# Second gate in three PSUM banks, three score slots in the dilated attention, and a transposition moved into the gate

## The chip, the cores and the metric

The kernel runs on one core of one Trainium2 chip as one launch of one program. The metric is the device time in microseconds; lower is better. Five engines work side by side, each through its own instructions in the order in which they are written, and wait for one another through counting semaphores: TensorE (PE in the profile; its weight loads are PEld), VectorE (DVE), ScalarE (ACT), GpSimd (POOL) and SyncE (SP), which issues most DMAs. TensorE writes only into PSUM, which has eight banks of 128 partitions by 512 floats.

## The reference

One inference step of a decoder layer for a prompt of 512 tokens and 8 samples of one token. All inputs go through one input projection, whose columns feed two attentions and four gates. The part that matters here is the dilated attention of the prompt (4 heads of 64, three patterns) and the gates beside it:

```python
h = _rms(x, norm_w) * (1 + scale[:, None]) + shift[:, None]
zq, zkv, zd, ga, gb, ma, mb, ... = split(h @ w_in)       # ga: 512 columns, gb: 256
...
for g, (win, dil) in enumerate(DIL_PATTERNS):            # (128,1), (512,4), (2048,16)
    s = einsum('bgnqhe,bgnkhe->bgnhqk', qb, kx) * DIL_SCALE
    s = where(band & has_prev, s, -inf)
    m = s.max(-1); e = exp(s - m[..., None]); l = e.sum(-1)
    acc = einsum('bgnhqk,bgnkhe->bgnqhe', e, vx)
o_b = _combine(stats).reshape(B, S, B_WIDTH)             # weighted by the softmax denominators
ya = (o_a * silu(ga)) @ w_pa
yb = (o_b * silu(gb)) @ w_pb
merged = sigmoid(ma) * ya + sigmoid(mb) * yb
y = x + res_gate * (merged @ w_out)
```

The 32 pages of each sample's cache, which the second half of the run works on, are not touched here.

## The kernel before

Every engine's instructions are written out by hand, in one order; semaphores carry the rest. The prompt half is a list of stages (STAGES). Each result tile of a stage has a running number, its item; item `idx` goes to PSUM bank `idx % 7`, and `wait_bank` lets TensorE write it once item `idx - 7` has been read out. Bank 7 is for odd jobs.

A projection (`block_of`) runs over chunks of 128 rows of the weight. Each chunk is loaded by SP into one of four raw slots, split by ACT (L620) and POOL (L931) into a high and a low part in one of three slots, and multiplied with the four tiles of 128 tokens and the tile of samples: three matmuls for each prompt tile, two for the samples, 14 in all per chunk. The gates are GA (512 columns) and GB (256 columns), of 8 chunks each.

Around the change the order on TensorE is: GA; the transposition of the third pattern's queries and keys (`heads_turned(2)`, stage TE, four items of four transposes); GB; the dilated attention (`pair_attention`); then the merge gates (MA0 and on). GA's tiles are read out by DVE (`mix`, L1927), which multiplies them with their sigmoid from ACT. TE's items are copied by ACT (`heads_in_order(2)`), GB's by ACT too.

The dilated attention has 16 jobs (PAIR_JOBS), each two heads of one tile of 128 queries: eight near jobs (first pattern; the first two have one block of keys, the others two), then eight far ones. A job n passes through:

- `qk(n)`, TensorE (L1255): scores of both heads, each into a bank of its own;
- `masks_max(n)`, DVE (L1895, L1900): adds the mask, takes the maximum, leaves the scores in `pair_probs`;
- `exp(n)`, ACT (L696);
- `tr(n)`, TensorE (L1266): transposes of the probabilities into a bank of PAIR_TURNED;
- `pt_copy(n)` (L469): that bank copied to `PT`, by DVE for even n and by ACT for odd n;
- PV(n), TensorE (L1297): probabilities times values, into a bank of PAIR_OUT;
- `finish(n)`, DVE (L1908): the result copied out.

Score slots, turned banks and output banks are two each. A turn of TensorE's loop is `tr(n + 1)`, `qk(n + 2)`, PV(n); a turn of DVE's is `masks_max(n + 1)`, `pt_copy(n)` if n is even, `finish(n - 1)`; a turn of ACT's is `exp(n + 1)`, `pt_copy(n)` if n is odd. `qk(0)` stands inside GB ahead of its chunk 5; `qk(1)` follows GB, since its banks hold GB's first two tiles.

Of the kernel before, what the change touches and what calls it, by code (L numbers as in the profile page):

```python
# [25 lines left out]
P = 128  # L26
# [65 lines left out]
FIRST = {}  # L92
# [47 lines left out]
_gb = [(ITEM["GB"] + t) % BANKS for t in range(BANKS)]  # L140
PAIR_SCORES, PAIR_OUT, PAIR_TURNED = ((_gb[5], _gb[6]), (_gb[0], _gb[1])), (_gb[3], _gb[4]), (7, _gb[2])
# [13 lines left out]
def turned_bank(chunk):  # L155

    return 6 + chunk % 2 if chunk < N_MLA_CHUNKS else PAIR_TURNED[(chunk - N_MLA_CHUNKS) % 2]
# [12 lines left out]
def trunk_step(nc, x_prompt, x_sample, cache_mla, cw0, cw1, cw2, page_table, c_prompt, c_sample, b_ada,  # L170
# [4 lines left out]
    with ctx:  # L175
# [154 lines left out]
        pair_p = v3(put("pair_probs", [P, 2 * 512], W + 18432), 2, 512)  # L330
# [272 lines left out]
        def _(act):  # L603
# [23 lines left out]
            def bank(idx, w, n=P, start=0):  # L627
                return ps[start:start + n, idx % BANKS, 0:w]
# [57 lines left out]
            def pair_attention():  # L686

                def exp(n):
                    near, i, hp, nb = PAIR_JOBS[n]
                    act.wait_ge(masked, N_MLA + n + 1)  # L690
                    for hh in range(2):
                        h = 2 * hp + hh
                        p = pair_p[:, n % 2, 256 * hh:256 * hh + nb * P]
# [319 lines left out]
        def _(pe):  # L1013
# [13 lines left out]
            def block_of(name, first, tiles, hi=None, lo=None, small=None, wait_h=False, ahead_of=None):  # L1027

                f, nk, w = FIRST[name], COUNT[name], WIDTH[name]
                for k in range(nk):  # L1030
# [8 lines left out]
                    for n, t in enumerate(tiles):  # L1039
# [3 lines left out]
                        out = ps[:, idx % BANKS, 0:w]  # L1043
                        st, en = k == 0, k == nk - 1
# [3 lines left out]
                        else:  # L1048
# [3 lines left out]
                            last = mm(out, lo[:, k, c], bh, start=False, stop=en)  # L1052
# [15 lines left out]
            def transposes(idx, parts, n_in=P):  # L1068

                wait_bank(idx)  # L1070
                for col, rows_out_, src in parts:
                    last = nc.tensor.transpose(ps[0:rows_out_, idx % BANKS, col:col + n_in], src, ident[0:n_in, 0:n_in])
                last.then_inc(z_done, 1)
# [165 lines left out]
            heads_turned(2, ITEM["TE"])  # L1239

            def pair_attention():
# [3 lines left out]
                def qk(n):  # L1245
                    near, i, hp, nb = PAIR_JOBS[n]
                    if n >= 2:
                        pe.wait_ge(masked, N_MLA + n - 1)
                    banks = PAIR_SCORES[n % 2]
# [9 lines left out]
                def tr(n):  # L1259
                    nb, c = PAIR_JOBS[n][3], N_MLA_CHUNKS + n  # L1260
                    pe.wait_ge(exp_done, N_MLA + n + 1)
                    if n >= 2:
                        wait_pt(pe, c - 2)
                    for q in range(2 * nb):
                        o = 256 * (q // nb) + P * (q % nb)
                        last = nc.tensor.transpose(ps[:, PAIR_TURNED[n % 2], q * P:(q + 1) * P], pair_p[:, n % 2, o:o + P], ident)  # L1266
# [12 lines left out]
                for n, (near, i, hp, nb) in enumerate(PAIR_JOBS):  # L1279
                    if n < last_job:  # L1280
                        tr(n + 1)
                    if n + 2 <= last_job:
                        qk(n + 2)
                    if n >= 2:
                        pe.wait_ge(o_done, N_MLA + n - 1)
# [5 lines left out]
                    for hh in range(2):  # L1291
                        h = 2 * hp + hh
                        for b in range(nb):
# [3 lines left out]
                            last = mm(ps[:, PAIR_OUT[n % 2], 64 * hh:64 * hh + 64], PT[:, c % 3, o:o + P], v_rows,  # L1297
# [207 lines left out]
        def _(dve):  # L1505
# [378 lines left out]
            def pair_attention():  # L1884

                def masks_max(n):
# [3 lines left out]
                    if n >= 2:  # L1890
                        dve.wait_ge(trp_done, N_MLA_CHUNKS + n - 1)
                    m = 4 * (n % 2)
                    msk = masks[:, M_ALL - w:M_ALL] if near else class_mask
                    for hh in range(2):
                        last = v.tensor_tensor_reduce(out=pair_p[:, n % 2, 256 * hh:256 * hh + w],  # L1895
                                                      in0=ps[:, PAIR_SCORES[n % 2][hh], 0:w], in1=msk, scale=1.0, scalar=NEG,
# [6 lines left out]
                def finish(n):  # L1903
# [4 lines left out]
                    v.tensor_copy(out, ps[:, PAIR_OUT[n % 2], 0:2 * DH].rearrange("p (h e) -> p h e", h=2)).then_inc(o_done, 1)  # L1908
# [366 lines left out]
```

## Time and profile before

| | |
|---|---|
| median of 3 runs | 1371.1 us (1368.76 to 1372.58) |
| profiled execution, its own time | 1372.51 us |
| its span, first to last instruction | 1370.7 us |
| mean granted TensorE clock | 0.913 of 2.4 GHz |
| busy share: PE, PEld, DVE, ACT, POOL | 89%, 73%, 52%, 36%, 19% |
| chain that ended last: PE, DVE, issue, ACT, DMA, POOL | 57%, 19%, 8%, 5%, 5%, 4% |

The profiled execution took 1.8 us beyond its span, and 1.4 us more than the median. The busy shares are means over stages with different limits. TensorE's clock has two levels, 2.4 and 1.2 GHz; a granted clock of 1.00 is the upper one, 0.50 the lower.

### The profile page before, as it was taken

Reading aid. Unit: us, or ns where it says so; the run is one execution under the profiler, and the core shown is the slowest. Engines: PE = TensorE matmul, PEld = TensorE weight load, DVE = VectorE, ACT = ScalarE, POOL = GpSimd, SP = SyncE. Lnnn points to the kernel's source line nnn. Section 1 sums busy time; section 2 is a strip of 40 time slices with the busy share of each in tenths; the row PEclk is TensorE's granted clock in tenths of the full one; section 3 lists DMA queues with packets and bytes.
Section 4 is the critical chain, followed back from the end, with each engine's and each line's share of the span. In section 5 each row is a group of like instructions: output and inputs, shape, how many; then the busy total and the mean of one; then the engine's idle time right before and its main releaser. Section 6 shows DMA issues by size and latency. Waiting matters only on the chain.

```text
span 1370.7 us, 22960 instructions
## 1 busy us (share of the span) xinstructions
PE 1219.1 (89%) x7616; PEld 998.1 (73%) x7616; DVE 715.8 (52%) x1657; ACT 495.2 (36%) x1159; POOL 254.7 (19%) x252
## 2 busy tenths in 40 slices
PE   5987758998897899999987999998999899997986
PEld 1277647786786678778765998988999899997431
DVE  4137887456865233030322676766676667676422
ACT  1133334332243333322322554545454545453010
POOL 0023330048865012333431000000000000000000
PEclk9989857999999657999998999999999999998579
DMA  8622010031242102233264310323232323225005
GB/s 262 220 77 72 23 41 1 13 81 47 73 127 77 31 23 71 77 101 85 71 199 159 96 31 22 88 62 88 61 86 64 88 61 83 66 75 184 1 20 166
DMA packets 79398, 112.24 MB, mean 82 GB/s; under 512 B 8627, under 2 KB 50756, under 8 KB 79293
## 3 DMA queue, kind: packets, MB, share of 16 engines
q1 hardware_dynamic: 76214, 101.59, 25.8%
q0 software_dynamic: 1440, 5.11, 1.0%
q10 hardware_dynamic: 1648, 4.23, 0.8%
q8 instruction: 65, 1.06, 0.3%
q14 instruction: 31, 0.25, 0.1%
HBM read 105.21 MB, written 5.68 MB: 81 GB/s over the span
## 4 chain that ended last, share of the span: by engine, by line
PE 57%; DVE 19%; issue 8%; ACT 5%; DMA 5%; POOL 4%; SPq 2%; ACTq 0%; DVEq 0%; POOLq 0%
PE ps L1376 18%; PE ps L1050 5%; PE ps L1051 5%; PE ps L1052 5%; PE ps L1357 5%; DVE ssq L2106 3%; PE ps L1065 3%; PE ps L1402 3%; DMA raw<-in_w_ada 2%; ACT cT_hi L850 2%; PE ps L1422 2%; PE ps L1212 1%; PE ps L1255 1%; POOL tmp L946 1%; PE ps L1266 1%
## 5 line engine op out<-in xcount | busy, mean ns | idle before, releaser
L931 POOL TENSOR_TENSOR wlo<-raw,whi 128x512 fp32r<-128x512 f32 (+3 forms) x148 | 172.1, 1165 | 459.8 <-ACT whi L620 459.6
L1376 PE MATMUL ps<-wq_hi,cT_hi 128*128 128x260 f32 x1024 | 217.8, 294 | 0.5 <-ACT sq L879 0.5
L1050 PE MATMUL ps<-whi,hT_hi 128*128 128x512 f32 (+3 forms) x512 | 190.3, 372 | 30.4 <-POOL wlo L931 19.2
L2106 DVE TENSOR_REDUCE ssq<-sq 128x8 f32<-128x512 f32 x256 | 172.6, 682 | 66.6 <-ACT sq L879 64.5
L1376 PE MATMUL ps<-wq_hi,cT_lo 128*128 128x260 f32 x1024 | 206.3, 283 | 0.0
L1376 PE MATMUL ps<-wq_lo,cT_hi 128*128 128x260 f32 x1024 | 206.0, 282 | 0.0
L620 ACT ACTIVATE whi<-raw 128x512 fp32r<-128x512 f32 (+3 forms) x148 | 83.3, 564 | 316.5 <-PE ps L1047 246.3
L1052 PE MATMUL ps<-whi,hT_lo 128*128 128x512 f32 (+3 forms) x512 | 185.8, 363 | 0.0
L1051 PE MATMUL ps<-wlo,hT_hi 128*128 128x512 f32 (+3 forms) x512 | 185.7, 363 | 0.0
L1376 PEld LDWEIGHTS ps<-wq_hi,cT_hi 128*128 128x128 f32 x1024 | 157.6, 190 | 1.1 <-ACT sq L879 1.1
L1376 PEld LDWEIGHTS ps<-wq_hi,cT_lo 128*128 128x128 f32 x1024 | 158.2, 189 | 0.0
L1376 PEld LDWEIGHTS ps<-wq_lo,cT_hi 128*128 128x128 f32 x1024 | 158.1, 189 | 0.0
L879 ACT ACTIVATE sq<-ps 128x512 f32<-128x512 f32 x256 | 152.0, 594 | 0.0
L1050 PEld LDWEIGHTS ps<-whi,hT_hi 128*128 128x128 f32 x512 | 99.2, 194 | 56.1 <-POOL wlo L931 25.3
L2024 DVE TENSOR_TENSOR cT_lo<-ps,cT_hi 128x1024 fp32r<-128x1024 f32 x64 | 78.3, 1224 | 103.3 <-ACT cT_hi L850 103.3
L1052 PEld LDWEIGHTS ps<-whi,hT_lo 128*128 128x128 f32 x512 | 98.9, 193 | 14.6
L1051 PEld LDWEIGHTS ps<-wlo,hT_hi 128*128 128x128 f32 x512 | 99.4, 194 | 13.4
L877 ACT ACTIVATE s_latent<-ps 128x8 f32<-128x8 f32 x256 | 45.2, 177 | 165.1 <-PE ps L1376 165.1
L850 ACT ACTIVATE cT_hi<-ps 128x1024 fp32r<-128x1024 f32 x64 | 65.7, 1027 | 83.5 <-PE ps L1359 83.4
L1357 PE MATMUL ps<-tab,cn 128*128 128x128 f32 x512 | 69.6, 280 | 17.5 <-DVE s_rotary L2103 10.1
L1357 PEld LDWEIGHTS ps<-tab,cn 128*128 128x128 f32 x512 | 55.5, 142 | 29.1 <-issue 24.6
L633 ACT ACTIVATE stage<-ps 128x512 f32<-128x512 f32 (+4 forms) x52 | 26.8, 556 | 120.1 <-PE ps L1065 97.7
(390 smaller groups left out, 1690.0 us busy)
## 6 DMA issues: line engine op xcount, KB each, us to landing
cn<-in_cache_mla SPq DMA_DIRECT2D x256, 144.0 KB, 2.1
raw<-in_w_in SPq DMA_DIRECT2D x64, 256.0 KB, 2.7
raw<-in_w_ada SPq DMA_DIRECT2D x48, 256.0 KB, 3.0
raw<-in_w_out SPq DMA_DIRECT2D x32, 256.0 KB, 3.0
sdk<-in_cw SPq DMA_DIRECT2D x3, 1536.0 KB, 11.0
raw<-in_w_in SPq DMA_DIRECT2D x32, 128.0 KB, 2.0
raw<-in_w_pa SPq DMA_DIRECT2D x16, 256.0 KB, 2.9
x_tiles<-in_x_prompt ACTq DMA_DIRECT2D x4, 512.0 KB, 5.6
```

The lines of the kernel that those rows point to most:

```text
L620: nc.scalar.activation(whi[:, s % NHL, 0:width], raw[:, j % NRAW, 0:width], ACT.Copy)\
L850: nc.scalar.activation(cThi[:, q % 2, :], psw(0, 1024), ACT.Copy).then_inc(ct_hi, 1)
L877: nc.scalar.activation(Sq[:, 4 * g + u, :].rearrange("p (f h) -> p f h", f=2), kb[:, :, s0:s0 + 4], ACT.Copy)
L879: nc.scalar.activation(sq4[:, u, :].rearrange("p (f n) -> p f n", f=2), kb[:, :, k0:k0 + 256], ACT.Square).then_inc(sq_done, 1)
L931: nc.gpsimd.tensor_tensor(out=wlo[:, s % NHL, 0:width], in0=raw[:, j % NRAW, 0:width], in1=whi[:, s % NHL, 0:width].bitcast(F32), op=ALU.s ...
L1050: mm(out, hi[:, k, c], bh, start=st, stop=False)
L1051: mm(out, hi[:, k, c], bl, start=False, stop=False)
L1052: last = mm(out, lo[:, k, c], bh, start=False, stop=en)
L1357: nc.tensor.transpose(ps[:, c, u * P:(u + 1) * P], src[:, c * P:(c + 1) * P], ident)
L1376: last = mm(ps[:, 3 + 2 * (u % 2) + f, 0:260], a[c], wq[:, c, f, w], start=c == 0 and a is hi and wq is wq_hi, stop=c == 1 and a is lo)
L2024: v.tensor_tensor(out=cTlo[:, q % 2, :], in0=psw(0, 1024), in1=cThi[:, q % 2, :].bitcast(F32), op=ALU.subtract)
L2106: v.tensor_reduce(out=ssq[:, (4 * g + u) * 8:(4 * g + u + 1) * 8], in_=sq4[:, u, :].rearrange("p (h e) -> p h e", e=NOPE), axis=AX, op=ALU ...
```

## The change

GB is packed: its four prompt tiles of 256 columns lie two to a bank in the banks `_ga[5]` and `_ga[6]`, and its tile of samples in bank 7. `_ga[t]` is the bank of GA's item t. So GB needs none of the banks that GA holds, and three banks instead of five. A table PLACE names the bank and column of the moved items, and HELD_BY the item that must have been read out first. TE's four items now take the banks of GA's four prompt tiles, and so wait for those.

On TensorE `heads_turned(2)` moves from before GB to before GB's chunk 2, and `qk(0)` and `qk(1)` stand before chunk 4. The attention's banks are dealt anew: three score slots of two banks (six banks), one turned bank and one output bank. `exp` and `masks_max` run two jobs ahead instead of one, TensorE's `qk` three instead of two. `tr(n)` waits for `pt_copy(n - 1)` instead of `pt_copy(n - 2)`, PV(n) for `finish(n - 1)` instead of `finish(n - 2)`. In DVE's loop `finish(n - 1)` now stands ahead of `pt_copy(n)`. ACT splits GB's chunks 3 and 4 ahead of TE's copies and the rest behind them. The third slot of `pair_probs` is 2 KB more of SBUF. The work itself, its instructions and their sizes, stays.

```diff
-_gb = [(ITEM["GB"] + t) % BANKS for t in range(BANKS)]
-PAIR_SCORES, PAIR_OUT, PAIR_TURNED = ((_gb[5], _gb[6]), (_gb[0], _gb[1])), (_gb[3], _gb[4]), (7, _gb[2])
+_ga = [(ITEM["GA"] + t) % BANKS for t in range(BANKS)]
+PAIR_SLOTS, PAIR_AHEAD = 3, 2
+PAIR_SCORES, PAIR_OUT, PAIR_TURNED = (_ga[0:2], _ga[2:4], _ga[5:7]), 7, _ga[4]
+PLACE = {ITEM["GB"] + t: (_ga[5 + t // 2], t % 2 * BW) for t in range(NT)}
+PLACE[ITEM["GBs"]] = (7, 0)
+SHARES_BANK = [ITEM["GB"], ITEM["GB"] + 2]
+HELD_BY = {ITEM["GB"] + t: ITEM["GA"] - 2 + t // 2 for t in range(NT)}
+HELD_BY[ITEM["GBs"]] = None
+for _t in range(4):
+    PLACE[ITEM["TE"] + _t], HELD_BY[ITEM["TE"] + _t] = (_ga[_t], 0), ITEM["GA"] + _t
...
-                split_to(FIRST["GB"] + COUNT["GB"])
-                exp(0)
+                for n in range(PAIR_AHEAD):
+                    exp(n)
                 act.wait_ge(far_stored[0], 16)
                 for t in range(NT):
+                    act.wait_ge(z_done, ITEM["GB"] + t // 2 * 2 + 2)
                     copy_out(ITEM["GB"] + t, gb_of[:, t, :], BW)
                 to_stage_small(ITEM["GBs"], BW, False)
                 for n in range(len(PAIR_JOBS)):
-                    if n + 1 < len(PAIR_JOBS):
-                        exp(n + 1)
+                    if n + PAIR_AHEAD < len(PAIR_JOBS):
+                        exp(n + PAIR_AHEAD)
...
             mix_gates("GA", AW)
+            split_to(FIRST["GB"] + 5)
             heads_in_order(2, ITEM["TE"])
+            split_to(FIRST["GB"] + COUNT["GB"])
             pair_attention()
...
-                if idx >= BANKS:
-                    wait_evac(pe, idx - BANKS)
+                held = HELD_BY.get(idx, idx - BANKS if idx >= BANKS else None)
+                if held is not None:
+                    wait_evac(pe, held)
...
             block_of("GA", ITEM["GA"], range(5), hThi, hTlo, hTs)
-            heads_turned(2, ITEM["TE"])
...
                     pe.wait_ge(exp_done, N_MLA + n + 1)
-                    if n >= 2:
-                        wait_pt(pe, c - 2)
+                    if n >= 1:
+                        wait_pt(pe, c - 1)
...
                 def first_scores(k):
-                    if k == 5:
+                    if k == 2:
+                        heads_turned(2, ITEM["TE"])
+                    elif k == 4:
                         wait_evac(pe, LAST_ITEM["TE"])
                         qk(0)
+                        qk(1)
 
                 block_of("GB", ITEM["GB"], range(5), hThi, hTlo, hTs, ahead_of=first_scores)
                 tr(0)
-                wait_evac(pe, ITEM["GB"] + 1)
-                qk(1)
+                wait_evac(pe, ITEM["GB"] + NT - 1)
+                qk(2)
                 wait_evac(pe, ITEM["GBs"])
                 for n, (near, i, hp, nb) in enumerate(PAIR_JOBS):
                     if n < last_job:
                         tr(n + 1)
-                    if n + 2 <= last_job:
-                        qk(n + 2)
-                    if n >= 2:
-                        pe.wait_ge(o_done, N_MLA + n - 1)
+                    if n + PAIR_SLOTS <= last_job:
+                        qk(n + PAIR_SLOTS)
+                    if n >= 1:
+                        pe.wait_ge(o_done, N_MLA + n)
...
-                masks_max(0)
+                for n in range(PAIR_AHEAD):
+                    masks_max(n)
                 take_small("GBs", mix_s[:, AW:768], BW)
                 for n in range(len(PAIR_JOBS)):
-                    if n + 1 < len(PAIR_JOBS):
-                        masks_max(n + 1)
+                    if n + PAIR_AHEAD < len(PAIR_JOBS):
+                        masks_max(n + PAIR_AHEAD)
+                    if n > 0:
+                        finish(n - 1)
                     if (N_MLA_CHUNKS + n) % 2 == 0:
                         pt_copy(dve, v.tensor_copy, N_MLA_CHUNKS + n, 2 * PAIR_JOBS[n][3], pt_d, ())
-                    if n > 0:
-                        finish(n - 1)
                 finish(len(PAIR_JOBS) - 1)
```

What stands in the order on three places follows; what an instruction waits for is in brackets. First TensorE between GA's last matmul (`hTs` x 512 columns) and GB's first chunks (256 columns); `dqn` and `kvo` are the third pattern's queries and keys, transposed for TE. Before:

```order
L1047 MATMUL ps<-wlo,hTs 128x512
L1072 MATMUL ps<-tab,dqn 128x128 [waits evac_a,rope_done]
L1072 MATMUL ps<-tab,dqn 128x128 x3
L1072 MATMUL ps<-tab,dqn 128x128 [waits evac_a]
L1072 MATMUL ps<-tab,dqn 128x128 x3
L1072 MATMUL ps<-tab,kvo 128x128 [waits evac_d]
L1072 MATMUL ps<-tab,kvo 128x128 x3
L1072 MATMUL ps<-tab,kvo 128x128 [waits evac_d]
L1072 MATMUL ps<-tab,kvo 128x128 x3
L1050 MATMUL ps<-whi,hT_hi 128x256 [waits evac_d,w_lo_ready]
L1051 MATMUL ps<-wlo,hT_hi 128x256
```

After, from the end of GB's chunk 1, whose 28 matmuls with chunk 0's follow GA directly:

```order
L1070 MATMUL ps<-wlo,hTs 128x256
L1095 MATMUL ps<-tab,dqn 128x128 [waits evac_d,rope_done]
L1095 MATMUL ps<-tab,dqn 128x128 x3
L1095 MATMUL ps<-tab,dqn 128x128 [waits evac_d]
L1095 MATMUL ps<-tab,dqn 128x128 x3
L1095 MATMUL ps<-tab,kvo 128x128 [waits evac_d]
L1095 MATMUL ps<-tab,kvo 128x128 x3
L1095 MATMUL ps<-tab,kvo 128x128 [waits evac_d]
L1095 MATMUL ps<-tab,kvo 128x128 x3
L1073 MATMUL ps<-whi,hT_hi 128x256 [waits w_lo_ready]
```

All four items now wait for DVE's reading of GA (`evac_d`), where before two of them did and GB's first two tiles did.

Second, one turn n of TensorE's attention loop among the far jobs, n even: `tr(n + 1)`, the scores, PV(n). `pt_d` counts DVE's copies of turned probabilities (even jobs), `pt_a` ACT's (odd jobs). Before:

```order
L1266 MATMUL ps<-tab,pair_probs 128x128 [waits pt_a,exp_done]
L1266 MATMUL ps<-tab,pair_probs 128x128 x3
L1255 MATMUL ps<-dkT,dqT 128x128 [waits masked]
L1255 MATMUL ps<-dkT,dqT 128x128 x3
L1297 MATMUL ps<-v_by_class,PT 128x64 [waits pt_d,o_done]
L1297 MATMUL ps<-v_by_class,PT 128x64 x3
```

After:

```order
L1289 MATMUL ps<-tab,pair_probs_135 128x128 [waits pt_d,exp_done]
L1289 MATMUL ps<-tab,pair_probs_135 128x128 x3
L1278 MATMUL ps<-dkT,dqT 128x128 [waits masked]
L1278 MATMUL ps<-dkT,dqT 128x128 x3
L1324 MATMUL ps<-v_by_class,PT 128x64 [waits pt_d,o_done]
L1324 MATMUL ps<-v_by_class,PT 128x64 x3
```

The order of the three groups stays; the transposes' wait moved from the copy of job n - 1 (`pt_a`) to that of job n (`pt_d`), the same that PV(n) waits for.

Third, an even turn of DVE's loop among the near jobs, from the second half of `masks_max` (ISA rows) on; L469 and L486 are `pt_copy`, L1908 and L1936 `finish`. Before:

```order
L1895 ISA pair_probs,amax<-ps,tab 128x256
L1895 ISA amax 128x1
L1900 TENSOR_SCALAR dil_stats<-amax 128x2 [waits dve_step]
L469 COPY PT<-ps 128x512 [waits pv_chunk,trp_done]
L1908 COPY oN<-ps 128x128 [waits pv_chunk]
```

After:

```order
L1923 ISA pair_probs_134,amax<-ps,tab 128x256
L1923 ISA amax 128x1
L1928 TENSOR_SCALAR dil_stats<-amax 128x2 [waits dve_step]
L1936 COPY oN<-ps 128x128 [waits pv_chunk]
L486 COPY PT<-ps 128x512 [waits pv_chunk,trp_done]
```

The copy of the turned probabilities moved behind the copy of the job before's result.

## Rows read from the trace of the kernel before

**Rows 1.** Page, granted clock in 40 slices of 34.3 us (tenths).

```profile
PEclk9989857999999657999998999999999999998579
```

**Rows 2.** Stretches: length, busy us of PE, PEld, DVE, ACT, POOL; clock; DMA.

```profile
430.26:436.61 6.35, 2.35 (x17) 1.66 (x16) 3.53 (x8) 6.03 (x11) 0.72 (x1) 0.99 0.66 190
436.61:443.30 6.69, 6.31 (x28) 6.02 (x29) 3.00 (x7) 1.24 (x3) 0.73 (x1) 0.50 0.04 9
443.30:454.00 10.70, 10.70 (x90) 10.45 (x90) 0.71 (x5) 4.88 (x13) 2.93 (x4) 1.00 0.39 106
454.00:457.30 3.30, 0.81 (x9) 0.48 (x7) 1.43 (x7) 1.91 (x7) 0.00 (x0) 0.94 0.00 0
461.30:524.40 63.10, 57.80 (x257) 45.85 (x257) 20.87 (x88) 21.94 (x65) 3.79 (x3) 0.50 0.05 13
```

**Rows 3.** Timeline, a turn of the attention loop; start, duration, engine, count, [idle before].

```profile
470.28 1.12 PE L1266 MATMUL ps<-tab,pair_probs 128*128 128x128 f32 x4 [0.31 <-ACT pair_probs L696]
471.33 1.23 PE L1255 MATMUL ps<-dkT,dqT 64*128 64x256 f32 x4
472.48 1.97 PE L1297 MATMUL ps<-kvo,PT 128*128 128x64 f32 x8
472.60 0.42 DVE L1895 CUSTOM_DVE_ANT_0 pair_probs<-ps,tab 128x256 f32<-128x256 f32 x1 [2.30 <-PE ps L1255]
...
473.49 0.69 DVE L469 COPY PT<-ps 128x512 f32<-128x512 f32 x1
473.62 0.51 ACT L696 ACTIVATE pair_probs<-pair_probs,dil_stats 128x256 f32<-128x256 f32 x1 [2.91 <-DVE dil_stats L1900]
...
474.49 0.29 DVE L1908 COPY oN<-ps 128x128 f32<-128x128 f32 x1 [0.31 <-PE ps L1297]
...
474.76 1.12 PE L1266 MATMUL ps<-tab,pair_probs 128*128 128x128 f32 x4 [0.31 <-ACT pair_probs L696]
...
478.09 0.51 ACT L696 ACTIVATE pair_probs<-pair_probs,dil_stats 128x256 f32<-128x256 f32 x1 [3.39 <-DVE dil_stats L1900]
...
479.09 0.57 ACT L469 ACTIVATE PT<-ps 128x512 f32<-128x512 f32 x1
```

**Rows 4.** Timeline of PE, GA's end to GB's end.

```profile
430.26 1.04 PE L1072 MATMUL ps<-tab,dqn 128*128 128x128 f32 x8
433.62 0.66 PE L1072 MATMUL ps<-tab,kvo 128*128 128x128 f32 x4 [2.32 <-DVE stage L1927]
435.07 0.66 PE L1072 MATMUL ps<-tab,kvo 128*128 128x128 f32 x4 [0.79 <-DVE stage L1927]
436.61 0.55 PE L1050 MATMUL ps<-whi,hT_hi 128*128 128x256 f32 x1 [0.89 <-DVE stage L1927]
...
437.97 0.58 PE L1050 MATMUL ps<-whi,hT_hi 128*128 128x256 f32 x1 [0.38 <-DVE stage L1927]
...
448.48 0.49 PE L1255 MATMUL ps<-dkT,dqT 64*128 64x128 f32 x4
```

**Rows 5.** Timeline, GB's end and the attention's start.

```profile
454.00 0.38 PE L1266 MATMUL ps<-tab,pair_probs 128*128 128x128 f32 x2
...
454.67 0.38 ACT L658 ACTIVATE low_s<-ps 8x256 f32<-8x256 f32 x1
455.08 0.41 DVE L1882 TENSOR_TENSOR mix_gates_s<-stage,low_s 8x256 f32<-8x256 f32 x1 [5.17 <-ACT low_s L658]
...
457.30 0.66 PE L1266 MATMUL ps<-tab,pair_probs 128*128 128x128 f32 x2 [2.49 <-ACT pair_probs L696]
```

**Rows 6.** Timeline of PE, the attention's end.

```profile
510.60 1.11 PE L1266 MATMUL ps<-tab,pair_probs 128*128 128x128 f32 x4 [0.31 <-ACT pair_probs L696]
...
524.37 0.80 PE L1050 MATMUL ps<-whi,hT_hi 128*128 128x512 f32 x1 [0.38 <-DVE o_by_class L1908]
```

**Rows 7.** Stretches of the first attention (four slots), as in Rows 2.

```profile
216.00:222.00 6.00, 5.98 (x27) 5.30 (x27) 4.26 (x28) 2.87 (x12) 0.00 (x0) 0.55 0.00 1
222.00:228.00 6.00, 5.20 (x35) 3.95 (x34) 5.08 (x29) 3.70 (x13) 0.00 (x0) 1.00 0.02 4
```

More of the change, by code:

```diff
@@ L155, in turned_bank @@
 def turned_bank(chunk):
-    return 6 + chunk % 2 if chunk < N_MLA_CHUNKS else PAIR_TURNED[(chunk - N_MLA_CHUNKS) % 2]
+    return 6 + chunk % 2 if chunk < N_MLA_CHUNKS else PAIR_TURNED
 N_MLA = len(MLA_JOBS)
@@ L329, in trunk_step @@
         gb_sig = v3(put("gate_b_sigmoid", [P, NT * BW], V + 16 * K1), NT, BW)
-        pair_p = v3(put("pair_probs", [P, 2 * 512], W + 18432), 2, 512)
+        assert 229344 - V >= 62 * K1 + 256, 229344 - V
+        pair_p = [put(f"pair_probs{n}", [P, 512], o)[:, :]
+                  for n, o in enumerate((W + 18432, W + 20480, V + 60 * K1 + 256))]
         st = put("dil_stats", [P, 160], W + 10240)
@@ L627, in bank @@
             def bank(idx, w, n=P, start=0):
-                return ps[start:start + n, idx % BANKS, 0:w]
+                b, c = place(idx)
+                return ps[start:start + n, b, c:c + w]
             def copy_out(idx, out, w, n=P, func=ACT.Copy):
@@ L1042, in block_of @@
                             wait_bank(idx)
-                        out = ps[:, idx % BANKS, 0:w]
-                        st, en = k == 0, k == nk - 1
+                        bank, col = place(idx)
+                        out = ps[:, bank, col:col + w]
+                        st, en = k == 0 and col == 0, k == nk - 1
                         if t == TS:
@@ L1051, in block_of @@
                             mm(out, hi[:, k, c], bl, start=False, stop=False)
-                            last = mm(out, lo[:, k, c], bh, start=False, stop=en)
+                            last = mm(out, lo[:, k, c], bh, start=False, stop=en and idx not in SHARES_BANK)
                         if en:
@@ L1071, in transposes @@
                 for col, rows_out_, src in parts:
-                    last = nc.tensor.transpose(ps[0:rows_out_, idx % BANKS, col:col + n_in], src, ident[0:n_in, 0:n_in])
+                    last = nc.tensor.transpose(ps[0:rows_out_, place(idx)[0], col:col + n_in], src, ident[0:n_in, 0:n_in])
                 last.then_inc(z_done, 1)
@@ L1246, in qk @@
                     near, i, hp, nb = PAIR_JOBS[n]
-                    if n >= 2:
-                        pe.wait_ge(masked, N_MLA + n - 1)
-                    banks = PAIR_SCORES[n % 2]
+                    if n >= PAIR_SLOTS:
+                        pe.wait_ge(masked, N_MLA + n - PAIR_SLOTS + 1)
+                    slot = n % PAIR_SLOTS
+                    banks = PAIR_SCORES[slot]
                     spans = [(0, i * P, (i + 1 - nb) * P, 0, nb * P)] if near else \
@@ L1296, in pair_attention @@
                                 vcl[:, b, i, h * 64:(h + 1) * 64]
-                            last = mm(ps[:, PAIR_OUT[n % 2], 64 * hh:64 * hh + 64], PT[:, c % 3, o:o + P], v_rows,
+                            last = mm(ps[:, PAIR_OUT, 64 * hh:64 * hh + 64], PT[:, c % 3, o:o + P], v_rows,
                                       start=b == 0, stop=b == nb - 1)
@@ L1889, in masks_max @@
                     dve.wait_ge(qk_done, N_MLA + n + 1)
-                    if n >= 2:
-                        dve.wait_ge(trp_done, N_MLA_CHUNKS + n - 1)
-                    m = 4 * (n % 2)
+                    if n >= PAIR_SLOTS:
+                        dve.wait_ge(trp_done, N_MLA_CHUNKS + n - PAIR_SLOTS + 1)
+                    slot = n % PAIR_SLOTS
+                    m = 4 * slot
                     msk = masks[:, M_ALL - w:M_ALL] if near else class_mask
                     for hh in range(2):
-                        last = v.tensor_tensor_reduce(out=pair_p[:, n % 2, 256 * hh:256 * hh + w],
-                                                      in0=ps[:, PAIR_SCORES[n % 2][hh], 0:w], in1=msk, scale=1.0, scalar=NEG,
+                        last = v.tensor_tensor_reduce(out=pair_p[slot][:, 256 * hh:256 * hh + w],
+                                                      in0=ps[:, PAIR_SCORES[slot][hh], 0:w], in1=msk, scale=1.0, scalar=NEG,
                                                       op0=ALU.add, op1=ALU.max, accum_out=amax[:, m + hh:m + hh + 1])
@@ L1907, in finish @@
                         else ocl[:, i, 2 * hp:2 * hp + 2, 0:DH]
[L1908 to L1910 removed]
+                    v.tensor_copy(out, ps[:, PAIR_OUT, 0:2 * DH].rearrange("p (h e) -> p h e", h=2)).then_inc(o_done, 1)
+                for n in range(PAIR_AHEAD):
+                    masks_max(n)
                 take_small("GBs", mix_s[:, AW:768], BW)
                 for n in range(len(PAIR_JOBS)):
[L1913 to L1914 removed]
+                    if n + PAIR_AHEAD < len(PAIR_JOBS):
+                        masks_max(n + PAIR_AHEAD)
+                    if n > 0:
+                        finish(n - 1)
                     if (N_MLA_CHUNKS + n) % 2 == 0:
                         pt_copy(dve, v.tensor_copy, N_MLA_CHUNKS + n, 2 * PAIR_JOBS[n][3], pt_d, ())
[L1917 to L1918 removed]
                 finish(len(PAIR_JOBS) - 1)
```

8 lines of the change are left out of this document (5 added, 3 removed).

## The prediction

> **What bounds it now.** I read the page's clock line first, then a table of stretches, then single turns on the timeline. The clock line [rows 1] shows the dilated attention at once: the slices 13 to 15 stand at 5 to 7 tenths, the longest stretch of the run at the lower clock. The table [rows 2] cuts that stretch into stages. From 430.26 to 436.61 TensorE is busy 2.35 of 6.35 us. From 436.61 to 443.30 GB runs at 1.2 GHz, from 443.30 to 454.00 at 2.4. From 461.30 to 524.40 the attention runs at 0.50 throughout, with TensorE busy 57.80 of 63.10 us (92%).
>
> One turn of its loop [rows 3] lasts 474.76 - 470.28 = 4.48 us: transposes 1.05 (to 471.33), scores 1.15 (to 472.48), PV 1.97 (to 474.45), and 0.31 of idling for ACT's exp. That wait ends a loop over three engines: scores done at 472.56, DVE's masks from 472.60, ACT's exp from 473.62, transposes at 474.76. So TensorE at its lower clock sets 4.17 us of the turn, and the two score slots 0.31.
>
> Ahead of it [rows 4] GA ends at 430.26, and TE and GB idle 2.32, 0.79, 0.89 and 0.38 us for DVE, which hands back GA's four banks one after the other (TensorE goes on at 433.62, 435.07, 436.61, 437.97). GB then starts slowly because its clock fell. Behind GB [rows 5] TensorE idles 2.49 us up to 457.30, as `qk(1)` could only be issued when GB had been read out, and the clock falls again.
>
> **GB and TE.** The order shows chunks 0 and 1 straight behind GA. GB's 90 matmuls between 443.30 and 454.00 take 10.70 us, 0.119 each, without an idle row [rows 2], so the feed by SP, ACT and POOL keeps that pace. Chunks 0 to 2 were split beside GA before and still are. 28 matmuls end at 430.26 + 3.33 = 433.6. Then TE's four items start as DVE frees GA's banks, whose times don't change: 433.62, 435.07, about 436.5, 437.97 [rows 4]. Four transposes take 0.52 (eight take 1.04), so TE ends at 438.5. Six chunks follow (84 x 0.119 = 10.0), with two score groups at 0.49: GB ends at 449.5 instead of 454.00. **Gain 4.5 us**, of which some 3.4 is that GB no longer runs 6.7 us at half clock.
>
> The moved waits: behind TE on TensorE stand chunk 2 and on; they have what they need by then. On ACT two splits stand ahead of TE's copies, and the rest behind them; the copies are wanted at chunk 4, some 3 us after TE. SP's and POOL's order is unchanged. The bound on the other side is the clock. TE is now spread over 4.9 us with three idle spells of about 0.9, and the same kind of stretch made it fall before (430.26 to 436.61, then 0.50 [rows 2]). Now two chunks stand in front of the spells, which makes it a near thing. If it falls, some 5 us of matmuls run at half speed: 2.5 less, a gain of 2.0. I take 4.5.
>
> **The turn of the attention.** The third slot takes exp off the path: it has a turn more. But the single turned bank makes `tr(n + 1)` wait for `pt_copy(n)`, and the order puts that copy late on both engines. From [rows 3], counted from the start of PV(n - 1), the time at which TensorE could next transpose being 1.97 later:
>
> - n odd, on ACT behind `exp(n + 2)`. The scores of n + 2 end 0.08 after that start, masks begin at 0.12, exp 1.02 later at 1.14, the copy 1.00 after exp starts (478.09 to 479.09), takes 0.57, and 0.05 later TensorE goes on: 2.76. Idle 0.79; the turn lasts 1.05 + 1.15 + 2.76 = 4.96.
> - n even, on DVE behind `finish(n - 1)`, which waits for PV(n - 1) itself. PV done at 1.97, the copy out at 2.01 (0.29, the next instruction starting about 0.08 before its end), `pt_copy` 0.69, and 0.05: 2.96. Idle 0.99; the turn lasts 5.16.
>
> The mean is **5.06 against 4.48**. The single output bank adds nothing: `finish(n - 1)` is over before PV(n) on both turns.
>
> A bank of its own per group is what a rule asks for. The Trainium skill, Perfetto Trace Analysis, section "Optimizing Tensor Performance", Matmuls, wants independent groups to rotate through PSUM banks so that evacuation of one overlaps the next. By it alone the exposed part of a turn would be the copy, 0.63 in the mean: 4.17 + 0.63 + 0.1 = 4.9, 4.2 us more over ten turns instead of 5.8. The rows put the cost elsewhere: transposes and copy take 1.8 of a turn, and would fit if the copy came at once.
>
> **Start and end.** GB's last copy by ACT ended 1.05 after GB (454.67 + 0.38); its pairwise waits may add 0.4. DVE's `take_small` (0.41 [rows 5]), `masks_max(2)` and the half-size `pt_copy(0)` (0.4, somewhat over half of 0.69) follow in its queue: 1.45 + 0.41 + 0.89 + 0.4 puts `tr(1)` 3.2 after GB, no earlier than now (3.30 [rows 5]). So the clock falls here again, I take it: TensorE has two transposes and one group of scores in 3.2 us, and then waits 2 us for `exp(3)` and the copy behind it. `tr(3)` comes 9.8 us after GB if the clock holds until then, 11.8 if it falls at once; I take 11.0. Ten turns at 5.06 bring `tr(13)` to 61.6. Then one turn of 4.96, one without scores (1.05 + 1.97 + 0.99 = 4.01), and 1.05 + 1.97 + 0.38 + 1.97 + 0.38 = 5.75 for the last two jobs, in which the single output bank costs 0.38: 76.3. Today it is 524.37 - 454.00 = 70.4, with `tr(13)` at 56.6 [rows 6]. **Loss 5.9 us.**
>
> **Sum.** -4.5 + 5.9 = +1.4. On the profiled execution's own 1372.5 that is 1373.9; on the median of 1371.1, which is 1.4 lower, **1372.5 us**. The merge gates behind the attention have their first chunks split in it as before, and what DVE and SP still do for it is covered by them, so nothing else moves.
>
> **The rivals.**
> *A, as above.* The clock stays up in GB, and falls as the attention starts: 1372.5, between 1371 and 1374.5 by the start (9.8 or 11.8).
> *B, the clock holds through the attention.* Its pieces on TensorE would halve (0.53, 0.58, about 1.0), while the loops over DVE and ACT stay: turns of 3.87 and 3.1, ten of 3.48, an end 54 us after GB: 16.5 saved and GB's 4.5, 1350. For it: the first attention rose to 2.4 GHz once it ran without idling (5.98 of 6.00 busy), and held with TensorE busy 5.20 of 6.00 [rows 7]. Against it: here the start idles as much as today, when the clock fell with an idle time of 2.49 us [rows 5]; and once down it did not come up in 63 us at 92% busy [rows 2], where the change leaves about 82%.
> The Trainium skill, TensorE: Matmul & The Clock Gate, section "Why this matters for your kernels", holds that only longer idle gaps than any here take the clock down; by it B would be the forecast. The trace disagrees: it fell in the 2.49 us.
> *C, the copies are not that late.* If DVE or ACT let `pt_copy` through in time, the turn is 4.48 as now or 4.17, with TensorE alone: GB's 4.5 and up to 4 more, 1362 to 1367. The order speaks against it: engines run in order.
> *D, slower: the clock falls between TE's items.* It decides at 436.5 to 438 us, with TE's idle spells of 0.9; once down, GB gains 2.0 only, and the attention still loses 5.9: 1375, up to 1377.5 with a late start. For it: the stretch in which it fell before has the same spells; against it: 28 matmuls without a gap ahead of them.
>
> **Chances and range.** A 0.52, D 0.24, C 0.14, B 0.10. A measurement of this kernel can tell about 0.3%, 4.1 us, from no change. Faster by more: B and most of C, 0.21. Slower by more than that, over 1375.2: the upper half of D and a little of A, 0.19. Within: 0.60. A range from 1364 to 1377 takes in A, nearly all of D and most of C, and leaves out B; A's own is 1371 to 1374.5.
>
> **What would show it.** In the changed kernel's rows: 28 matmuls of GB behind GA without a gap; TE's items released by DVE at 433.6, 435.1, 436.5, 438.0; GB's end near 449.5, and the granted clock 1.00 from 438 to there (0.50 would be D). In the attention TensorE's idle time before the transposes put down to the copies into PT, about 0.8 and 1.0 in turn, with the exp no longer named; turns of about 5.0 and 5.2; clock 0.50. I'm wrong if the clock shows 1.00 in the attention, if the turns are at 4.5 or less, or if GB ends after 453.

## The result, and the profile after

The changed kernel takes **1373.51 us** (median of nine runs, 1372.09 to 1378.69), the kernel before 1368.76 beside it (nine runs): a ratio of 1.003, with an interval of 1.0016 to 1.0044. That is about 4 us more, where 1.4 more was forecast.

The page's clock line of the changed kernel looks like that of before [rows 1]; the long stretch at the lower clock is still there.

```profile
PEclk9988857999999657999998999999999999998588
```

Cut into stretches as in [rows 2] (columns as there), it shows where the 4 us come from. GA ends 1.57 us earlier in this execution, at 428.69; over the twelve profiled executions of this study its end lies anywhere from 427.72 to 432.89, so lengths count here and not positions.

```profile
428.69:435.30 6.61, 5.08 (x40) 4.50 (x39) 3.79 (x8) 5.76 (x11) 1.67 (x3) 1.00 0.62 184
435.30:442.00 6.70, 6.08 (x29) 5.69 (x28) 2.75 (x7) 2.33 (x5) 1.64 (x2) 0.50 0.24 61
442.00:450.26 8.26, 8.26 (x72) 8.01 (x71) 1.29 (x10) 4.47 (x14) 1.47 (x2) 0.99 0.35 95
450.26:461.56 11.30, 6.01 (x31) 3.65 (x29) 4.66 (x20) 4.86 (x17) 0.00 (x0) 0.74 0.00 0
461.56:524.59 63.03, 50.92 (x233) 41.45 (x233) 17.78 (x74) 18.40 (x57) 3.80 (x3) 0.50 0.05 13
```

From GA's end to GB's end is now 450.26 - 428.69 = 21.57 us; before it was 454.00 - 430.26 = 23.74. **GB gives 2.2 us.** It ran the 6.70 us of the second row at 1.2 GHz. (2.2 is the gain of this execution: five kernels below leave GB as it is here, and took 19.0 to 21.6 for it.) The attention, from GB's end to the next gate's first matmul, takes 526.94 - 450.26 = 76.68; before 524.37 - 454.00 = 70.37. **It costs 6.3 us.** The sum is +4.1, and the ratio gives the same. (The two spans, 1370.7 and 1372.3, lie only 1.6 apart, since GA's end is 1.57 earlier here and what follows the attention 0.97 shorter.) TensorE's busy share in the attention's loop fell from 57.80 of 63.10 us to 50.92 of 63.03.

TE's four items, on TensorE's timeline, answer to [rows 4]. They come 3.45, 4.81, 6.26 and 7.71 us after GA's end, three of them behind an idle spell that DVE ends. The last takes 1.12 for its four transposes where the first takes 0.63: the clock fell between them.

```profile
432.14 0.63 PE L1095 MATMUL ps<-tab,dqn 128*128 128x128 f32 x4
433.50 0.66 PE L1095 MATMUL ps<-tab,dqn 128*128 128x128 f32 x4 [0.73 <-DVE stage L1956]
434.95 0.83 PE L1095 MATMUL ps<-tab,kvo 128*128 128x128 f32 x4 [0.80 <-DVE stage L1956]
436.40 1.12 PE L1095 MATMUL ps<-tab,kvo 128*128 128x128 f32 x4 [0.62 <-DVE stage L1956]
```

Two turns of the attention's loop, on the timeline of three engines, answer to [rows 3].

```profile
466.58 1.09 PE L1289 MATMUL ps<-tab,pair_probs 128*128 128x128 f32 x4 [0.88 <-ACT PT L486]
467.60 1.22 PE L1278 MATMUL ps<-dkT,dqT 64*128 64x256 f32 x4
...
468.75 1.97 PE L1324 MATMUL ps<-kvo,PT 128*128 128x64 f32 x8
468.87 0.42 DVE L1923 CUSTOM_DVE_ANT_0 pair_probs<-ps,tab 128x256 f32<-128x256 f32 x1 [2.84 <-PE ps L1278]
...
470.75 0.29 DVE L1936 COPY oN<-ps 128x128 f32<-128x128 f32 x1 [0.91 <-PE ps L1324]
...
470.96 0.68 DVE L486 COPY PT<-ps 128x512 f32<-128x512 f32 x1
...
471.79 1.09 PE L1289 MATMUL ps<-tab,pair_probs 128*128 128x128 f32 x4 [1.07 <-DVE PT L486]
...
473.96 1.97 PE L1324 MATMUL ps<-kvo,PT 128*128 128x64 f32 x8
...
475.10 0.51 ACT L714 ACTIVATE pair_probs<-pair_probs,dil_stats 128x256 f32<-128x256 f32 x1 [4.12 <-DVE dil_stats L1928]
...
476.10 0.57 ACT L486 ACTIVATE PT<-ps 128x512 f32<-128x512 f32 x1
...
476.81 1.09 PE L1289 MATMUL ps<-tab,pair_probs 128*128 128x128 f32 x4 [0.88 <-ACT PT L486]
```

The transposes had ended by 467.67, and the copy that frees their bank starts at 470.96, when DVE is through with the masks (from 468.87) and with `finish` (470.75), which waits for PV. On the other turn ACT has been free since 470.98, and copies only at 476.10, because it first does an exp whose scores end at 474.0 and whose masks follow. TensorE waits 1.07 us for DVE's copy in one turn and 0.88 for ACT's in the next; the exp is named no more. The turns last 5.21 and 5.02.

Three of the kernels below took 20 to 27 us longer in one or two of six executions (copies first 1353.01 and 1355.84 us, copies first and spread 1349.81 and 1352.86, first copy ahead of small 1355.09); the ratios leave those out, the medians do not, and the last experiment's profile shows one.

### The profile page after: what moved, and what is told of

It reads as the page before. It is cut to its first block, busy times and chain, and to the rows that moved or that the text cites. A ratio compares the mean times of both kernels' runs of the same rounds, so it can differ in the third digit from the quotient of the medians.

```text
span 1372.3 us, 22963 instructions
## 1 busy us (share of the span) xinstructions
PE 1210.7 (88%) x7616; PEld 995.1 (73%) x7616; DVE 715.6 (52%) x1657; ACT 495.1 (36%) x1159; POOL 255.3 (19%) x252
## 4 chain that ended last, share of the span: by engine, by line
PE 57%; DVE 19%; issue 8%; DMA 5%; ACT 5%; POOL 4%; SPq 2%; ACTq 0%; DVEq 0%; POOLq 0%
PE ps L1403 18%; PE ps L1073 5%; PE ps L1074 5%; PE ps L1075 5%; PE ps L1384 5%; DVE ssq L2135 3%; PE ps L1429 3%; PE ps L1088 3%; DMA raw<-in_w_ada 2%; ACT cT_hi L871 2%; PE ps L1449 2%; DMA raw<-in_w_out 2%; PE ps L1235 1%; POOL tmp L967 1%; PE ps L1241 1%
```

## The experiments

**Theory.** The attention is slower because the copies into PT stand late in DVE's and ACT's queues, where the single turned bank makes TensorE wait for them at once; the banks themselves cost nothing. GB gives only 2.2 because the clock falls in the idle spells between TE's items. **Rivals:** one turned and one output bank cost the time, wherever the copies stand; or GB's clock falls anyway.

In the table "GB" is GA's end to GB's end and "attention" GB's end to the next gate, both on TensorE in the profiled execution; the clock is that of most of the attention. The last row's stages are those of an execution in which the clock fell.

| kernel | ratio to before, interval | GB, us | attention, us | clock |
|---|---|---|---|---|
| before | 1 | 23.7 | 70.4 | 0.50 |
| the change | 1.0030, 1.0016 to 1.0044 | 21.6 | 76.7 | 0.50 |
| DVE's copy ahead of `finish` | 0.9983, 0.9974 to 0.9992 | 21.6 | 69.1 | 0.50 |
| ACT's copy ahead of exp | 0.9957, 0.9941 to 0.9973 | 20.3 | 68.4 | 0.50 |
| copies first on both | 0.9726, 0.9711 to 0.9740 | 21.6 | 36.2 | 1.00 |
| copies first for jobs 0 and 1 only | 1.0006, 0.9994 to 1.0017 | 19.0 | 73.4 | 0.50 |
| copies first from job 3 on | 0.9925, 0.9906 to 0.9944 | 21.6 | 62.1 | 0.50 |
| gate alone | 0.9954, 0.9942 to 0.9967 | 19.9 | 67.6 | 0.50 |
| items spread | 0.9996, 0.9985 to 1.0008 | 16.4 | 76.7 | 0.50 |
| gate alone, items spread | 0.9931, 0.9915 to 0.9946 | 16.6 | 67.6 | 0.50 |
| copies first, items spread | **0.9681**, 0.9663 to 0.9698 | 16.7 | 36.3 | 1.00 |
| the same, first copy ahead of small | 0.9705, 0.9686 to 0.9724 | 16.4 | 58.0 | 0.50 |

### DVE's copy ahead of finish

The order of the kernel before, on DVE alone:

```diff
                         masks_max(n + PAIR_AHEAD)
-                    if n > 0:
-                        finish(n - 1)
                     if (N_MLA_CHUNKS + n) % 2 == 0:
                         pt_copy(dve, ...)
+                    if n > 0:
+                        finish(n - 1)
```

> Changed kernel, with one thing different: in DVE's loop of the dilated attention the copy into PT comes ahead of finish again. Theory (the place of the copies in DVE's and ACT's queues costs the turn): the turns that idled 1.07 us for DVE lose that idle time, since the copy can start when masks_max is over, about 1.0 us into a PV of 1.97: 4.17 instead of 5.22. The others stay at 5.02. The mean is 4.6 instead of 5.12, some 6 us less over twelve turns: about 1367.5. Rival (the single turned bank or the single output bank costs it, wherever the copy stands): turns of 5.0 to 5.2 as now, 1373.5.

It came out as the theory has it: 1367.64 us. On TensorE's timeline every other turn is free of waiting and lasts 4.02; the one that waits for ACT is unchanged at 5.02.

```profile
465.77 1.09 PE L1289 MATMUL ps<-tab,pair_probs 128*128 128x128 f32 x4 [0.88 <-ACT PT L486]
...
469.79 1.09 PE L1289 MATMUL ps<-tab,pair_probs 128*128 128x128 f32 x4
...
474.81 1.08 PE L1289 MATMUL ps<-tab,pair_probs 128*128 128x128 f32 x4 [0.88 <-ACT PT L486]
```

### ACT's copy ahead of exp

```diff
+                    if (N_MLA_CHUNKS + n) % 2:
+                        pt_copy(act, ...)
                     if n + PAIR_AHEAD < len(PAIR_JOBS):
                         exp(n + PAIR_AHEAD)
-                    if (N_MLA_CHUNKS + n) % 2:
-                        pt_copy(act, ...)
```

> The counterpart of DVE's copy first: only ACT's copy stands ahead of its exp, DVE's stays last. Theory at 1.2 GHz: the turns that idled 0.88 us for ACT lose that, 4.17 instead of 5.02; the others stay at 5.22; mean 4.7, some 5 us less: 1368.5. ACT's late copy is also the longest idle time at the start (2.12), so if that one takes the clock down, it holds at the start; then the turns with DVE's copy behind finish still idle, and whether the clock lasts is open: 1350 if it does.

The counterpart holds: the waits for ACT are gone, those for DVE still stand at 1.07, and turns last 3.93 and 5.19.

```profile
460.32 1.09 PE L1289 MATMUL ps<-tab,pair_probs 128*128 128x128 f32 x4 [1.07 <-DVE PT L486]
...
464.25 1.06 PE L1289 MATMUL ps<-tab,pair_probs 128*128 128x128 f32 x4
...
469.44 1.09 PE L1289 MATMUL ps<-tab,pair_probs 128*128 128x128 f32 x4 [1.07 <-DVE PT L486]
```

The expectation was 3.5 us too high (1365.05), for two reasons: 3.93, not 4.17, and a start without the 2.12 us of waiting for ACT's copy. The clock still fell at the start, just behind the 1.82 us of waiting ahead of `tr(1)`.

### Copies first on both engines

ACT as in the last edit, and on DVE:

```diff
+                    if (N_MLA_CHUNKS + n) % 2 == 0:
+                        pt_copy(dve, ...)
                     if n + PAIR_AHEAD < len(PAIR_JOBS):
                         masks_max(n + PAIR_AHEAD)
                     if n > 0:
                         finish(n - 1)
-                    if (N_MLA_CHUNKS + n) % 2 == 0:
-                        pt_copy(dve, ...)
```

> Changed kernel, with the copies into PT ahead of everything else on both engines: on DVE ahead of masks_max and finish, on ACT ahead of exp. One turned bank and one output bank as in the change. Theory: no turn idles for a copy, turns of 4.17 at 1.2 GHz, 0.95 less than now in each of twelve: about 1362. If TensorE, once it runs without idle time, is granted 2.4 GHz, the turn falls towards 3 us and the time to 1345 to 1352. Rival (the banks cost it): turns stay at 5.0 to 5.2 and the time at 1373. A second rival: the copies push masks and exp back so far that exp ends the wait before the transposes, as in the kernel before: turns of about 4.5, 1366.

Far beyond the expected 1345 to 1352: 1334.53 in the median. It has the single turned and the single output bank of the change, so those are not what the change lost. TensorE's timeline of the start shows why the step is this large:

```profile
454.75 0.41 PE L1289 MATMUL ps<-tab,pair_probs 128*128 128x128 f32 x2 [0.93 <-DVE PT L486]
...
457.17 0.63 PE L1289 MATMUL ps<-tab,pair_probs 128*128 128x128 f32 x4 [0.79 <-ACT PT L486]
...
458.86 0.61 PE L1289 MATMUL ps<-tab,pair_probs 128*128 128x128 f32 x4
...
481.54 0.61 PE L1289 MATMUL ps<-tab,pair_probs 128*128 128x128 f32 x4
```

The spells of the start are 0.93 and 0.79 where the change has 1.81 and 2.12, and the clock does not fall in the attention: from 458.86 to 481.54 ten turns take 22.68 us, 2.27 each, at a granted clock of 1.00. Two of these ten still wait 0.26 for ACT's copy, so at this clock the single bank is not quite free.

### Copies first only at the start, or only behind it

The same edits under a condition on the job, `n < 2` for the one kernel and `n > 2` for the other (ACT's part for `n < 2`; DVE's is alike):

```diff
+                    if (N_MLA_CHUNKS + n) % 2 and n < 2:
+                        pt_copy(act, ...)
                     if n + PAIR_AHEAD < len(PAIR_JOBS):
                         exp(n + PAIR_AHEAD)
-                    if (N_MLA_CHUNKS + n) % 2:
+                    if (N_MLA_CHUNKS + n) % 2 and not n < 2:
                         pt_copy(act, ...)
```

> Changed kernel, with the copies first only for the jobs 0 and 1, from which the idle times at the attention's start come (1.81 and 2.12 us in the change); from job 2 on they stand late as in the change. Theory S (the start decides the clock; once it is held, idle times of a turn don't take it down): granted clock 1.00 in the attention, turns of 3.9 and 3.1 as worked out for rival B, an end some 54 us after GB: 1348 to 1352. Rival (every turn has to be nearly free of idle time, as with copies first): the clock falls within the first turns, since at 2.4 GHz the late copies leave 1.0 to 1.8 us idle in each; then turns of 5.12, and only the 2 us of the start are gained: 1369 to 1372.

Theory S fell; 1370.77 us is its rival's time. The clock stays at 1.00 through the shortened start, and falls in the first spell that a late copy makes, 1.38 us ahead of `tr(3)` (its transposes take 1.08 again, on TensorE's timeline):

```profile
454.13 0.63 PE L1291 MATMUL ps<-tab,pair_probs 128*128 128x128 f32 x4 [0.79 <-ACT PT L486]
...
457.36 1.08 PE L1291 MATMUL ps<-tab,pair_probs 128*128 128x128 f32 x4 [1.38 <-DVE PT L486]
```

In GB this execution shows something else. Its gate is the change's, TE's items stand behind the same spells (0.73, 0.80 and 0.80), and yet the clock stays at 1.00 and GB takes 19.02. The last two items, and the row of the granted clock around them:

```profile
436.65 0.66 PE L1097 MATMUL ps<-tab,kvo 128*128 128x128 f32 x4 [0.80 <-DVE stage L1960]
438.11 0.66 PE L1097 MATMUL ps<-tab,kvo 128*128 128x128 f32 x4 [0.80 <-DVE stage L1960]
...
436.00:440.00 4.00, 2.55 (x20) 2.31 (x21) 3.73 (x8) 2.59 (x5) 1.75 (x2) 1.00 0.44 120
```

> The opposite: the start as in the change (copies of the jobs 0 to 2 late, the clock falls there), copies first from job 3 on. Theory S: the clock falls at the start as in the change; then turns without idle time, 4.17 us at 1.2 GHz. If it stays down: twelve turns at 0.95 less, 1362. If running without idle time brings it back after some us, as in the first attention (93% busy before, 100% when it rose), turns of 2.1 to 2.5 from there: 1340 to 1350. Rival (the order of the copies alone gives what copies first gave): 1334.

The clock falls at the start as in the change, and then stays down, although TensorE hardly idles. These are two stretches, the start and what follows:

```profile
449.31:460.60 11.29, 6.00 (x30) 3.64 (x29) 4.67 (x20) 4.85 (x17) 0.00 (x0) 0.74 0.00 0
464.54:509.10 44.56, 44.18 (x217) 37.59 (x217) 17.41 (x69) 17.85 (x53) 3.79 (x3) 0.50 0.07 18
```

Turns last 3.90, which gives 1359.3:

```profile
464.54 1.06 PE L1291 MATMUL ps<-tab,pair_probs 128*128 128x128 f32 x4
...
466.68 1.97 PE L1326 MATMUL ps<-kvo,PT 128*128 128x64 f32 x8
468.44 1.06 PE L1291 MATMUL ps<-tab,pair_probs 128*128 128x128 f32 x4
```

Copies first lies some 42 us under the change (1.0030 to 0.9726). About 14 of these (1.0030 to 0.9925) come at the lower clock, by the order in the loop alone; the rest comes with the start, whose spells are shorter and whose clock holds. The clock needs both: the short start to be kept and the order in the loop to last.

### The gate alone

GB packed, TE and the first two groups of scores in it; the attention with two score slots, two turned and two output banks and the old order. This is the deal of banks:

```diff
-PAIR_SLOTS, PAIR_AHEAD = 3, 2
-PAIR_SCORES, PAIR_OUT, PAIR_TURNED = (_ga[0:2], _ga[2:4], _ga[5:7]), 7, _ga[4]
+PAIR_SLOTS, PAIR_AHEAD = 2, 1
+PAIR_SCORES, PAIR_OUT, PAIR_TURNED = (_ga[0:2], _ga[2:4]), _ga[5:7], (_ga[4], 7)
```

> GB alone: GB packed in three banks, TE inside it and the first two score groups ahead of its last chunk as in the change, but the attention with two score slots, two turned banks, two output banks and the order of the kernel before. Theory: GB's stage gains the 2.2 us that it gains in the change, and the attention's turns are those of before, 4.48: 1366.5, up to 3 us less if the earlier scores shorten the start. Rival (the packing costs something that the attention hides in the change): 1368.8 or more.

1363.86 us, at the lower end of what was expected. GB gains 3.8 us in this execution (the clock falls among TE's items as in the change, but comes back after some 3.5 us and not after 6.7), and the attention gains 2.8, since `qk(1)` no longer waits for GB to be read out. No cost of the packing shows. This half of the change is a gain by itself; the attention's half gives it away.

### Items spread over GB

Two of TE's items move ahead of chunk 3, two ahead of chunk 4, and the first scores ahead of chunk 5 (the helper's new argument is left out here):

```diff
-                    if k == 2:
-                        heads_turned(2, ITEM["TE"])
-                    elif k == 4:
+                    if k in (3, 4):
+                        heads_turned(2, ITEM["TE"], range(2 * k - 6, 2 * k - 4))
+                    elif k == 5:
```

> Changed kernel, with TE's four items spread over GB: two ahead of chunk 3, two ahead of chunk 4, and the scores ahead of chunk 5. Theory (the clock falls in the three idle spells of 0.6 to 0.8 us between TE's items): GB's banks from GA have been freed when the items come, no idle spell, the granted clock stays at 1.00 through GB, and GB ends 3 to 5 us earlier: 1369 to 1370.5. Rival (the clock falls anyway, or something else than the spells takes it down): GB ends where it does now, 1373.5.

The spells are gone, and the clock stays up. In the stretch from the end of chunk 2 to GB's end the granted clock is 1.00 with TensorE busy 11.17 of 11.40 us:

```profile
434.00:445.40 11.40, 11.17 (x96) 10.67 (x95) 6.23 (x20) 7.64 (x22) 3.58 (x5) 1.00 0.43 130
445.40:456.70 11.30, 6.42 (x30) 4.01 (x29) 4.76 (x20) 4.86 (x17) 0.00 (x0) 0.69 0.00 0
```

The time is 1369.91 us, as expected. GB takes 16.40 us, 5.2 less than in the change, and the attention is unchanged at 76.70. Beside the 19.02 of copies first for jobs 0 and 1 only, which has the spells but not the fall, this splits the 5.2: 2.6 are the spells, 2.6 the lower clock. In all four profiled executions without the spells (this one and the three kernels below) GB's clock is 1.00; in the seven with them it fell in six, for 3 to 7 us. So the spells let the clock fall, but not each time; what decides between the two stays open.

### Gate alone, items spread

Both edits above in one kernel.

> GB alone with the items spread: packed banks and TE in GB, two ahead of chunk 3 and two ahead of chunk 4; the attention with two score slots, two turned and two output banks, as in the kernel before. Theory (the edits act apart; the attention with two slots stays at 1.2 GHz because exp ends the wait before each group of transposes): turns of 4.48, and 3.6 us less than GB alone: 1360. Rival (a shorter start is all that the attention needs for 2.4 GHz): 1330 to 1340.

1360.95 us, and turns of 4.48 at a clock of 0.50, each with its 0.31 for the exp: the two parts add up. A start whose spells are 0.93, 1.62 and 1.17 does not hold the clock here.

### Copies first and items spread

> Both edits in one kernel: copies into PT first on DVE and ACT, and TE's items spread over GB. Theory (the two act apart): GB's stage gains the 3.6 us that spreading alone gave, on top of copies first: 1331 from 1334.5, or from the 1332 to 1336 of most of its executions. Rival (the start of the attention then has its idle times so placed that the clock falls there): 1350 to 1360.

The best kernel of this study, **1326.91 us in the median**, 3.2% under the kernel before (0.9681, 0.9663 to 0.9698), and 4 us below the 1331 expected. The clock is 1.00 in all three stretches: GB, the attention's start, its loop.

```profile
428.24:444.89 16.65, 16.41 (x137) 15.68 (x136) 8.24 (x24) 12.22 (x29) 4.86 (x6) 1.00 0.49 144
444.89:453.66 8.77, 6.68 (x46) 4.35 (x45) 5.60 (x26) 5.32 (x19) 0.00 (x0) 1.00 0.00 1
453.66:479.65 25.99, 24.93 (x216) 20.82 (x216) 19.11 (x69) 17.30 (x54) 3.80 (x3) 1.00 0.12 32
```

### First copy ahead of take_small

The last kernel, with one move on DVE at the start, where `pt_copy(0)` had stood behind the sum of the samples' rows:

```diff
-                take_small("GBs", mix_s[:, AW:768], BW)
                 for n in range(len(PAIR_JOBS)):
                     if (N_MLA_CHUNKS + n) % 2 == 0:
                         pt_copy(dve, ...)
+                    if n == 0:
+                        take_small("GBs", mix_s[:, AW:768], BW)
```

> Copies first and items spread, and DVE copies PT of job 0 ahead of take_small, which it waits for until ACT has read GB's rows. Theory (which way the attention starts decides the clock of the whole attention): tr(1) follows qk(2) at once, so the idle time of 0.93 before it goes, but tr(2) still waits for exp(2), so most of it returns there: one spell of some 1.5 us instead of 0.93 and 0.79, 0.4 us less in sum. If the clock holds, 1326; if the longer spell takes it down more often, most executions at 1350. Rival (what takes it down in a third of the executions is not in the start): the same mix as without this edit.

No gain: five of six executions lie at 1324.97 to 1332.33, as without the move. The sixth, at 1355.09, is the profiled one, and shows what happens in such an execution. On TensorE's timeline `tr(1)` follows at once and `tr(2)` waits 1.43, as expected; just behind that spell the clock falls, and the rest of the attention runs at 0.50 although TensorE is busy 50.84 of 51.23 us:

```profile
450.00 0.44 PE L1289 MATMUL ps<-tab,pair_probs 128*128 128x128 f32 x2
...
453.08 0.76 PE L1289 MATMUL ps<-tab,pair_probs 128*128 128x128 f32 x4 [1.43 <-ACT PT L486]
```

```profile
448.69:453.08 4.39, 2.68 (x18) 1.49 (x17) 2.87 (x13) 2.86 (x10) 0.00 (x0) 1.00 0.00 0
453.08:504.31 51.23, 50.84 (x244) 42.32 (x245) 20.29 (x81) 20.88 (x64) 3.79 (x3) 0.50 0.06 16
```

So the start sits on an edge: the same program keeps its clock in most executions and loses it in some. One of six against two of six is too few to say whether one longer spell is better than two shorter ones; that stays open.

## Why the prediction was right, and where it was wrong

**The time** was right, 1372.5 forecast and 1373.51 measured, but one step in it failed, and its size was covered by the range. That the two lie 1 us apart is in part luck: the forecast stood on a median before of 1371.1, and the kernel before took 1368.76 beside the changed one. As a difference, +1.4 was forecast and +4.1 came, which is the sum of rival D (5.9 less 2.0, +3.9). The upper ends that the prediction gives A and D, 1374.5 and 1377.5, are wider than its sums: a start of 11.8 instead of 11.0 adds 0.8, which makes 1373.3 and 1375.8.

**GB and TE.** The order and the waits came as forecast: 28 matmuls behind GA, then items at 3.45, 4.81, 6.26 and 7.71 us after GA's end, where 3.4, 4.8, 6.2 and 7.7 were read from [rows 4]. What failed is "I take 4.5": that 28 matmuls without a gap would carry the clock over the three spells. It fell at about 435.3, as rival D (chance 0.24) had it, and GB gained 2.2 where D had 2.0. The size of the fall was right, 2.6 us between 21.57 and the 19.02 of the execution whose clock stayed up behind the same spells, for the 2.5 of the prediction. That execution gained 4.7, so A's 4.5 is what GB gives when the clock holds, and "a near thing" was well said; but it fell in six of seven executions, and the like stretch in [rows 2] was the better guide.

**The turn of the attention** was right in mechanism and near in size. Idle 0.88 behind ACT's copy and 1.07 behind DVE's were forecast at 0.79 and 0.99, turns of 5.02 and 5.21 at 4.96 and 5.16. The difference is one term: the prediction puts 0.05 between a copy's end and the transposes, and it was 0.14 behind ACT's (476.10 + 0.57 to 476.81) and 0.15 behind DVE's (470.96 + 0.68 to 471.79). The two single-engine edits took away one wait each and left the other as it was. Ten turns from 461.56 to 512.73 take 51.2 (50.6 forecast), `tr(3)` comes 11.3 us after GB (11.0), and the single output bank costs 0.39 before the last PV, where 0.38 was said. The loss was 6.3 for 5.9. With GB's 2.2 for 4.5 that makes +4.1 instead of +1.4.

**The banks.** The prediction put the cost in the place of the copies and not in the number of banks. With the copies first and the same single banks the turn at 1.2 GHz is 3.90, below the 4.48 of two turned banks before (where 0.31 is the wait for exp, with two score slots, and none is for a bank). That is less than the prediction's floor of 4.17, mostly because without a wait the transposes start 1.76 us after PV does (466.68 to 468.44) and not 1.97. The rule on rotating banks (the Trainium skill, Perfetto Trace Analysis, "Optimizing Tensor Performance", Matmuls), as the prediction applied it to the turned bank, would have had 4.9; here one bank was enough at this clock once its copy came at once, since the copy is over while the scores and PV fill other banks. Two turned banks with the copies first were not run, nor copies first in the kernel before.

**Rival C** (copies in time) did not happen in the change, but copies first from job 3 on gave what it priced and more, 1359.3.

**Rival B** (the clock holds) was rightly set aside for this change: with the late copies the clock fell even when the start had been shortened for it. What the prediction did not price is that another place for two calls would have held it in most executions, at 1331 to 1336. It looked for the price of the late copies in idle time alone, some 6 us; with the clock they cost about 42.

## What to carry to other kernels

When a change gives a bank or a slot less to one stage, look first at where the instruction that frees it stands in its engine's queue: put the copy that the next group waits for ahead of work that is wanted a turn later. When two stages share one chain, test the halves apart, since a gain of 6 us in one was hidden by a loss in the other. And where a stretch stands at the lower clock, price what idle time costs by the clock too: the spells that begin a stage can decide the speed of all of it.

## What the runs showed of the hardware that was not expected

- The clock stayed at 1.2 GHz for 44.56 us with TensorE busy in 44.18 of them (copies first from job 3 on), and for 51.23 us with 50.84 busy (the last kernel). The same loop, with the clock kept at its start, ran at 2.4 GHz with TensorE busy 24.93 of 25.99 us. So two speeds of one loop last here, and what happens at its start picks one. The prediction had read from [rows 7] that the first attention "rose to 2.4 GHz once it ran without idling"; these runs speak against that for this loop. Why the first attention rose and this one did not stays open. The Trainium skill, TensorE: Matmul & The Clock Gate, section "Why this matters for your kernels", names keeping TensorE busy as the way to the higher clock. By that rule these stretches would have risen, and the traces disagree.
- The clock fell with three spells of 0.73, 0.80 and 0.62 us between groups of four transposes in GB, and with one of 1.38 behind the attention's start. With 0.73, 0.80 and 0.80 in GB it stayed in one execution, and with two of 0.93 and 0.79 at the attention's start in most. The same section names only longer gaps than these as its danger; the traces disagree here too.
